# Six projections of a hybrid mixer as three float32r products, and modulation loads moved one step later in the load order

## What is computed

```python
h = modulate(x, hyb_norm, shift, scale)             # rmsnorm(x) * (1 + scale) + shift, 256 x 1024
q, k, v, lowrank, r, qb, kv, gates = split_cols(h @ hyb_w_in, HYB_SPLITS)
# q, k 256 columns each, v and r 512: gated linear attention, 4 heads, chunks of 64 tokens
# qb 512, kv 768, gates 24: sparse attention, 8 heads (compressed, selected, window)
x = x + gate * (concat(gla(q, k, v, lowrank, r), nsa(qb, kv, gates)) @ hyb_w_out)
# every sublayer has its own modulation: silu(c) @ mod_w + mod_b -> shift, scale, gate
```

## Time and profile before

| what | value |
|---|---|
| median of 3 executions | 2768.37 us (2762.62 to 2768.43) |
| the profiled execution's own time | 2768.21 us |
| its span, first to last instruction | 2766.2 us |
| PE busy | 2674.8 us, 97% |
| DVE, ACT, POOL busy | 44%, 28%, 2% |
| mean granted clock of PE | 0.982 |
| hybrid mixer, from projection 6 to the norm of the dense sublayer | 75 to 211 us |

### The profile page before, as it was taken

The page is one execution under the profiler, slowest core; times in us unless marked ns, Lnnn a source line. Parts: engine busy times, 40 slices in busy tenths (PEclk is TensorE's granted clock), DMA queues, the critical chain, the costliest instruction groups (busy, mean ns, idle before and its releaser), DMA issues.

```text
span 2766.2 us, 50434 instructions
## 1 busy us (share of the span) xinstructions
PE 2674.8 (97%) x22522; PEld 1921.0 (69%) x22522; DVE 1230.5 (44%) x1976; ACT 763.9 (28%) x1184; POOL 56.9 (2%) x39
## 2 busy tenths in 40 slices
PE   8999999999999999999999999999999999999998
PEld 6789997878433333333333646799999987798998
DVE  3367773454301101101101396455555586665554
ACT  2334332353200000000000203334444454212443
POOL 0000000000000000000000000000000000231000
PEclk9999999999999999999999999999999999999999
DMA  9856765545899999999999424355554440002451
GB/s 381 317 226 262 276 256 213 212 169 237 337 385 421 420 420 420 421 421 420 420 420 421 183 86 154 136 226 217 197 183 183 153 168 31 2 19 107 184 184 45
DMA packets 95199, 686.91 MB, mean 248 GB/s; under 512 B 10624, under 2 KB 11776, under 8 KB 11904
## 3 DMA queue, kind: packets, MB, share of 16 engines
q1 hardware_dynamic: 94400, 681.35, 62.3%
q10 hardware_dynamic: 576, 2.26, 0.2%
HBM read 682.52 MB, written 1.05 MB: 247 GB/s over the span
## 4 chain that ended last, share of the span: by engine, by line
PE 84%; DVE 5%; DMA 5%; SPq 3%; ACT 2%; issue 1%; POOL 0%; DVEq 0%; ACTq 0%; POOLq 0%
PE ps L539 40%; PE ps L2203 14%; PE ps L951 12%; PE ps L2228 5%; PE ps L831 5%; DMA ring<-W 4%; SPq L3873 3%; PE ps L552 2%; PE ps L2231 2%; PE ps L1691 1%; PE ps L804 1%; DMA AR<-W 1%; PE ps L2211 1%; ACT AR L1884 0%; DVE RN L775 0%
## 5 line engine op out<-in xcount | busy, mean ns | idle before, releaser
L2203 PE MATMUL ps<-AR 128*32 128x512 f32 x2520 | 404.4, 593 | 11.5 <-DMA AR<-W 5.9
L539 PE MATMUL ps<-FR,FR 128*128 128x256 f32 x3120 | 387.5, 284 | 0.3 <-DVE FR L903 0.3
L539 PEld LDWEIGHTS ps<-FR,FR 128*128 128x128 f32 x3120 | 378.8, 192 | 3.4 <-issue 3.3
L903 DVE TENSOR_TENSOR FR<-ring,FR 128x2048 fp32r<-128x2048 f32 x129 | 294.1, 2291 | 140.2 <-ACT FR L887 139.0
L951 PE MATMUL ps<-FR,FR 128*128 128x256 f32 x2832 | 349.0, 283 | 0.0
L2203 PE MATMUL ps<-ring,AR 128*32 128x512 f32 x1960 | 344.5, 592 | 3.5 <-DMA ring<-W 2.1
L951 PEld LDWEIGHTS ps<-FR,FR 128*128 128x128 f32 x2832 | 343.9, 192 | 0.0
L2323 DVE TENSOR_TENSOR AR<-AR,ps 128x256 f32<-128x256 f32 x70 | 29.6, 423 | 676.0 <-ACT AR L2286 360.3
L539 PE MATMUL ps<-HT,ring 128*128 128x256 f32 (+1 forms) x1108 | 286.1, 418 | 0.8 <-issue 0.8
L887 ACT ACTIVATE FR<-ring 128x2048 fp32r<-128x2048 f32 x129 | 244.5, 1908 | 98.1 <-PE ps L951 81.9
L2203 PEld LDWEIGHTS ps<-AR 128*32 128x32 f32 x2520 | 110.4, 110 | 221.1 <-issue 218.3
(11 more groups left out here) (473 smaller groups left out, 2976.0 us busy)
## 6 DMA issues: line engine op xcount, KB each, us to landing
ring<-W SPq DMA_DIRECT2D x457, 1024.0 KB, 6.6
AR<-W SPq DMA_DIRECT2D x189, 1024.0 KB, 24.4
XT<-XIN ACTq DMA_DIRECT2D x2, 1024.0 KB, 8.8
cst<-CS SPq DMA_DIRECT2D x1, 1843.0 KB, 19.1
out<-XT SPq DMA_DIRECT2D x4, 256.0 KB, 2.2
sml<-SM SPq DMA_DIRECT2D x1, 970.5 KB, 15.1
cst<-CS ACTq DMA_DIRECT2D x1, 144.5 KB, 7.7
sml<-SM ACTq DMA_DIRECT2D x1, 16.0 KB, 5.3
```

What stands on the lines that cost most here:

```text
L539: ins = g.matmul(out, l, r, **kw)
L903: g.tensor_tensor(lo, src, hi.bitcast(F32), SUB).then_inc(*s.done(self.x + ".lo", i, frees=sl))
L2203: ins = g.matmul(bank.ap[group(i), :], mo.hg[e % 2][:, 4 * h + k, group(t)], w[n][:, k, :], start=j == 0 and k == 0, stop=j == 1 and k == ...
```

## The change

Six of the twelve projections (6 to 11) are made as three float32r products. h gets a high part `hy.hhi` in `HT[:, :, 256:512]` (ACT) and a low part `hy.hlo` in `XT[:, 1]` (DVE), which is the place of the context; the context's load, on ACT's queue, now waits for projection 11. The six loads get a high part (ACT, `make_act`) in free parts of the mixer's memory and a low part in place (DVE, `make_dve`), at fixed points of both programs. `hybrid_steps(4)` becomes 1 where it was 2, so from there on every modulation step stands one step later in the load order. The steps on PE and DVE stay where they are.

```diff
 def hybrid_steps(u):
-    return 0 if u < 2 else 2 if 4 <= u < 8 else 1
+    return 0 if u < 2 else 2 if 5 <= u < 8 else 1
...
+        hy.hhi, hy.hlo = HT_low[:, :, 256:512], XT_low[:, 1, :, :]
...
+        hy.high_at = {HY_K: mark_ - 2048, HY_Q: sc_at + 4096, HY_V: mark_ - 2048, HY_V + 1: sc_at + 4096, HY_R: mark_ - 2048, HY_R + 1: mark_}
...
+        hy.names = [("hyb_in", u) for u in (HY_K, HY_Q, HY_V, HY_V + 1, HY_R, HY_R + 1)]
+        def hybrid_high(i):
+            at = hy.high_at[hy.names[i][1]]
+            free = {2: [("hy.in", HY_K)], 3: [("hy.in", HY_Q)], 4: [("hy.in", HY_V)], 5: [("hy.kte",), ("hy.kd",), ("hy.qd",)]}
+            return hy.low[:, at:at + 2048], free.get(i, [])
+        def hybrid_splits():
+            return InPlace("hy", hy.names, hybrid_high, None, from_ring)
...
+            def begin3(u):
+                n = hy.names.index(("hyb_in", u))
+                b = counts.take("hy.in", u)
+                s.wait_emptied(b).wait_ge("hy.hlo").wait_ge("hy.lo", n)
+                return w.pair(n), b
+            def rows3(u):
+                pair, b = begin3(u)
+                for h in range(2):
+                    ins = up3(g, pair, (hy.hhi, hy.hlo), h * 128, b.ap[:, h * 256:h * 256 + 256])
+                ins.then_inc(*s.done("hy.in", u, frees=(slot("hyb_in", u),)))
...
             for u in (HY_K, HY_Q):
-                rows(u)
+                rows3(u)
                 bg.go(2)
             scores(0, 0)
             scores(0, 1)
-            tokens(HY_V)
+            tokens3(HY_V)
...
-            tokens(HY_V + 1)
+            tokens3(HY_V + 1)
...
-            rows(HY_R)
+            rows3(HY_R)
...
-            rows(HY_R + 1)
+            rows3(HY_R + 1)
# ACT
+            s.own().activation(hy.hhi, HT[:, :, 0:256], ACT.Copy).then_inc(*s.done("hy.hhi"))
...
             keys_values(HY_SLC)
+            w.make_act(g, s, 1)
...
             keys_values(HY_WIN)
+            w.make_act(g, s, 3)
             exps(0, 0)
             exps(0, 1)
             tokens(HY_V)
+            w.make_act(g, s, 4)
...
             exps(1, 0)
+            w.make_act(g, s, 5)
             tokens(HY_V + 1)
...
+            w.make_act(g, s, 6)
             exps(1, 1)
# DVE
             queries(1)
+            s.wait_ge("hy.hhi")
+            g.tensor_tensor(hy.hlo, HT[:, :, 0:256], hy.hhi.bitcast(F32), SUB).then_inc(*s.done("hy.hlo"))
             bg.go(7)
+            w.make_dve(g, s, 2)
...
             bg.go()
+            w.make_dve(g, s, 3)
...
             scores(0, 1)
             bg.go()
+            w.make_dve(g, s, 4)
             scores(1, 0)
...
+            w.make_dve(g, s, 5)
             bg.go(2)
             scores(1, 1)
...
+            w.make_dve(g, s, 6)
...
         def dense_act(g, s):
+            s.wait_ge("hy.in", HY_R + 1)
             g.dma_start(XT[:, 1, :, :], XIN[1]).then_inc(s_in["ctx"], 16)
```

More of the change, by code:

```diff
@@ L459, in program @@
         sml = sb("sml", [128, nsm])
+        with ExitStack() as first:
+            XT_low = first.enter_context(nc.sbuf_tensor("XT_low", [128, 2, 8, 256], F32R))
         XT = sb("XT", [128, 2, 8, 256])
@@ L970, in softplus @@
             s.own().scalar_tensor_tensor(out=x, in0=x, scalar=0.0, in1=q, op0=MAX, op1=ADD).then_inc(*s.done("plus"))
+        HY_LOW, HY_CMP, HY_QB, HY_SLC, HY_WIN, HY_K, HY_Q, HY_V, HY_R = 0, 1, 2, 4, 5, 6, 7, 8, 10
         hy = Stage()
         m_ = memory(1, 25900)
+        with ExitStack() as first:
+            hy.low = first.enter_context(nc.sbuf_tensor("hy_low", [128, 25900], F32R))
+        hy.hhi, hy.hlo = HT_low[:, :, 256:512], XT_low[:, 1, :, :]
         hy.qd = m_.get(512, "p (k t) -> p k t", k=2)
@@ L999, in program @@
         hy.vcz = m_.get(512, "p (h d) -> p h d", h=8)
+        sc_at = m_.at
         hy.sc = [[m_.get(1024 * (q + 1), "p (h k) -> p h k", h=8) for _ in range(2)] for q in range(2)]
@@ L1018, in program @@
         hy.bend = hy.t2.rearrange("p k (n c) -> p (k n) c", c=64)[:, :, 63:64]
-        HY_LOW, HY_CMP, HY_QB, HY_SLC, HY_WIN, HY_K, HY_Q, HY_V, HY_R = 0, 1, 2, 4, 5, 6, 7, 8, 10
+        hy.names = [("hyb_in", u) for u in (HY_K, HY_Q, HY_V, HY_V + 1, HY_R, HY_R + 1)]
[5 more added lines that the diff above has]
+            return InPlace("hy", hy.names, hybrid_high, None, from_ring)
         def pair2(ps):
@@ L1044, in rows, with tokens3 @@
                 ins.then_inc(*s.done("hy.in", u, frees=(i,)))
-            def tokens(u):
-                i, b = begin(u)
+            w = hybrid_splits()
+            def begin3(u):
[8 more added lines that the diff above has]
+                ins.then_inc(*s.done("hy.in", u, frees=(slot("hyb_in", u),)))
+            def tokens3(u):
+                pair, b = begin3(u)
+                v = [q.rearrange("p (k c) -> p k c", k=8) for q in pair]
                 for x in range(2):
-                    ins = proj_tm(g, i, 0, 256, b.ap[:, x * 256:x * 256 + 256], x * 128)
-                ins.then_inc(*s.done("hy.in", u, frees=(i,)))
+                    t = slice(x * 128, x * 128 + 128)
+                    ins = mm(g, b.ap[:, x * 256:x * 256 + 256],
+                             [q for k in range(8) for q in three([hy.hhi[:, k, t], hy.hlo[:, k, t]], [v[0][:, k, :], v[1][:, k, :]])])
+                ins.then_inc(*s.done("hy.in", u, frees=(slot("hyb_in", u),)))
             def keys_values(u):
```

## The result

| kernel | median, us | lowest to highest | executions |
|---|---|---|---|
| before | 2765.77 | 2762.62 to 2768.43 | 6 |
| after | 2776.56 | 2773.91 to 2780.93 | 6 |

The account below looks back on a forecast made before the run. PE, busy 97% of the span, was taken to bound the kernel. Matmuls -7.5, waits +2.65 and +1.0, projection 11 +1.25 gave -2.6; the residual's +3.5 made +0.9 on 2768.21, so 2769 us, range 2761 to 2775.

Parts of the forecast that it names:

- The wait before projection 6: Hybrid mixer: PE waits 2.65 us for DVE's low part, which stands behind the closing step of hyb_gate.
- The old wait: Before projection 9: PE's 3.88 us wait for a load would become a 4.9 us wait at `hy.at`.
- No later load was waited for: Dense and state space sublayers: modulation loads one step later keep 3 us of cover, at no cost.
- At the output product the kernel is 2.6 us early: End of the mixer: of 7.5 us saved by the matmuls, 2.6 us would be left.
- six products: Projections 6 to 11: each saves PE 1.25 us as float32r matmuls, 7.5 us together.
- half clock around projection 9, less the 2.8 of before: Projection 9: the low clock after the wait was taken again, with no change in its cost.
- projection 11: wait behind DVE, or half clock: Before the output product: projection 11's 1.25 us is lost, as PE waits some 1.6 us behind DVE's chain.
- The landing of hyb_in 9: Load for projection 9: issued at 102.2, landing at about 108.6 us, 7.6 us earlier than before.
- rival 3: Projection 6: new idle time brings the low clock, +2 to +5 us, total 2771 to 2774; chance 0.15.
- Late by 3.5 us: Norm before the first dense product: late ssm_mod 4, landing at 198.7, delays DVE's residual and the norm by 3.5 us.
- the low clock that follows this idle time I take as it was: Norm at the mixer's end: half clock after PE's wait was assumed unchanged, adding nothing to the sum.
- Slower by over 0.2%: Whole kernel: a time slower than 2773.9 us, from rival 3's upper end and spread; chance 0.12.

Follow-up runs that it names:

- c8: Kernel after with ssm_mod 4 ahead of the last hyb_out, low parts of projections 6 earlier and 9 later on DVE, load hyb_in 9 earlier; 2762.38 us, 0.9980 of before.
- c1: Kernel after with the load ssm_mod 4 put back ahead of the last hyb_out; 2772.12 us, 1.0014 of before.
- c4: Kernel after with the load order of before, so the products alone; 2774.42 us, 1.0029 of before.
- c6: c1 with DVE's low part of projection 9 moved behind the reading of scores(1, 0); 2766.97 us, 0.9998 of before.
- c2: Kernel before with the new load order alone, all twelve projections in float32; 2769.96 us, 1.0007 of before.
- c3: c2 with the load ssm_mod 4 put ahead of the last hyb_out; 2760.40 us, 0.9971 of before.
- c9: c3 with 48 small float32 matmuls added on PE near 11 us, results unread; 2764.35 us, 0.9990 of before.
- c11: c8 with projections 10 and 11 back in float32 and their splits left away; 2764.79 us, 0.9998 of before.
- c5: c1 with DVE's low part of projection 6 moved ahead of the closing step of hyb_gate; 2765.86 us, 0.9996 of before.

## Why the prediction was wrong

**What held.** The wait before projection 6 (2.65 said, 2.56 seen, for DVE's low part). The old wait moved to `hy.at` and was ended by the reading at L1411 (4.9 said, 5.95 seen). A float32r projection costs 5.9 us. The four passes that the Trainium skill gives a true FP32 product ("FP8 and Floating Point Precision", section "TensorE Precision Notes") would by my estimate have made it 5.3 us; the rows after disagree, at 5.9, as those of before did. No later load was waited for up to 680 us, though every modulation load comes one step later. ssm_mod 4 was issued at 190.15 + 1.97 = 192.12 in the time of before (192.2 said).

**"At the output product the kernel is 2.6 us early".** The change earned 1.03. The terms, from the rows above (a plus is time lost):

| term | said | measured |
|---|---|---|
| six products | -7.5 | -7.5 |
| wait before projection 6 | +2.65 | +2.56 |
| wait at `hy.at` less the old one of 3.88 | +1.0 | +2.07 |
| half clock on projection 6 | 0 | 7.19 - 5.85 = +1.34 |
| half clock around projection 9, less the 2.8 of before | 0 | 8.91 - 7.01 - 2.8 = -0.9 |
| projection 11: wait behind DVE, or half clock | +1.25 | 7.38 - 5.85 = +1.53 |
| sum | -2.6 | -0.9 |

(5.85 is a projection at full clock: 80.54 - 74.71 = 5.83 and 114.17 - 108.3 = 5.87 in c8; 8.91 is 125.39 - 116.48, and 7.01 is 1.16 + 5.85.) Two terms failed, and one came right by luck. The landing of hyb_in 9 took 7.3 us from its issue, not the 6.4 that lay in 108.6 - 102.2; the chain behind it, 116.48 - 110.0 = 6.5, was as said (6.35). And the granted clock was under 1 between 76.5 and 80: that was rival 3's test. I had given rival 3 one chance in seven, because 2.54 us of idle time before 495.7 had not brought it. Here 2.56 us of idle time was followed by it, in after, in c1 and in c4; its price was 1.3 us, not the 2 to 5 I gave it, so rival 3 alone would not have moved the forecast out of its range. The luck is projection 11. I had said that PE would wait 1.6 us for DVE's chain behind it; the kernel after has no such wait, and lost nearly the same time to half clock. That wait shows in c6, at 1.44 us.

**"Late by 3.5 us".** It was 8.46, the largest miss. 1.6 is the landing: 198.36 + 1.97 = 200.33 against 198.7. 3.0 is the norm's matmuls, 6.61 in place of 3.62, at half clock; the small rest stands in the chain from the residual to the norm. The step that failed is "the low clock that follows this idle time I take as it was". Before, PE came to the norm without idle time, and its matmuls were over when the clock fell. A later residual made PE idle for 5.31 us ahead of them, so the half clock moved onto them. c2 against c3 is the test with nothing else changed: one load's place, 7.7 us from the output product to the first dense product. c1 shows that it was also the larger part of the loss of the kernel after, 7.5 us by the ratios. (The prediction also says that DVE would idle for about 3 us for this load. Its own times give 198.7 - 192.46 = 6.2, and 7.81 were measured.)

**What the sum had no term for.** About 4.5 us at 2486 us, and 1.7 more between 218 and 2475. The first is the late low clock. That products are not needed for it is shown by c9. That it goes with a longer PE program rests on the count of traces: it is in the profiles of all nine kernels with products (22586 to 22618 matmuls) and of c9, and in none of before, c2 and c3 (22522). The 180 instruction packets of the page against 179 don't explain it, since c11 has 179 and the low clock. What in the longer program makes the clock fall, its length or where its parts come to lie, stays open. So does how often it does so: c1's eleven executions fall into five of 2768.1 to 2769.6 us at a mean clock of 0.979 to 0.980 and six of 2772.1 to 2773.6 at 0.977, a distance that fits one such stretch, but only one execution of each kernel has a trace.

**The chances.** Slower by over 0.2% had 0.12. I had let one row of half clock move, in rival 3, and held all others fixed. Of the 12.6 us of the profiled execution, 3.0 + 1.34 - 0.9 + 1.53 + 1.7 + 4.5 = 11.2 are put down to half clock (the 1.7 by the windows of half clock that after has and before has not, near 430 and 503 us), and 1.4 is everything else, beside +0.9 in the sum.

**The better kernel.** The load order of the change with ssm_mod 4 back ahead of the last hyb_out, and no products, is c3: 0.9971 (0.9959 to 0.9983). With six products and all but one of their new waits removed, c8 gives 0.9980 (0.9970 to 0.9991). The intervals overlap, so which of the two is faster is not shown; in the profiles the products are worth 4.1 us at the end of the stage and lose them again in clock by the end.

## What to carry to other kernels

Count a wait of PE twice: for itself, and for the matmuls that will stand behind it if the clock falls; look which these are after the change, not before. In a ring with strict order, find for each moved load the consumer that is followed by the longest chain to PE, and keep that one where it was: here one load's place decided 7.7 us (c2 and c3) and 8.5 us (after and c1) of 2770. Before a difference between two traces is put down to a change, look whether they already differ ahead of it: c2 and c3 do, by 1.6 us of half clock. A gain of a few microseconds in one stage should be read at the stage's end and again at the kernel's end, since the clock far behind it can change too, here in a kernel that differed only by 48 matmuls near its start.

## What the hardware showed that was not expected

- The granted clock fell to half in a stretch where PE was busy for 11.00 of 11 us (2486 to 2497, matmuls of 64x64), after idle times of 0.33 and 0.62 us that are the same in kernels where it did not fall. In the traces, c9 had this stretch and c3 had not, and they differ by 48 matmuls without use 2460 us earlier; it cost 4.5 us.
- With the same PE program and the same loads up to there, the clock fell at 139.7 us in c2 and stayed full in c3: 8.66 us against 7.10 for projection 11, counted from start to start.
- Idle time of 2.56 us (after, c1, c4), of 1.97 us before projection 9 in c6, and none at all at 144.7 us was each followed by 3.4 to 6.8 us at half clock; 3.88 us of idle time in the kernel before was too, and 2.54 before 495.7 was not, though in the kernel after the same place was (0.57 on the mean of 503 to 507 us). So the length of an idle time alone did not decide it.
- A load of 1 MB landed 4.8 us after its issue (dense_mod 5), 7.3 (hyb_in 9 behind it) and 8.2 (ssm_mod 4, with two loads under way ahead of it). hyb_in 9 itself took 6.3 us before, 7.3 after, 6.2 in c1 and 8.4 in c5, so a landing is no constant even for one load.
